# Earlier weights for the first pair, and an earlier eviction of the ninth product, in a one-core hybrid block kernel

## The reference, cut to what matters

```python
h = rmsnorm(x, norm_pre) * (1.0 + scale) + shift
proj = h @ w_in                       # 1024 x 1024 times 1024 x 6144
u_pool, z_pool, u_ssm, z_ssm, g_pool, g_ssm = split(proj)
y_pool = causal_pool_mixer(u_pool, pool_w, pool_scale) * silu(z_pool)
y_ssm = s5_mixer(u_ssm, ...) * silu(z_ssm)   # complex-diagonal state space
merged = sigmoid(g_pool) * (y_pool @ w_branch_pool) + sigmoid(g_ssm) * (y_ssm @ w_branch_ssm)
return x + gate * rmsnorm(merged @ w_out, norm_post)
```

## Time and profile before

| | |
|---|---|
| device time, median of 3 (lowest, highest) | 975.13 us (974.8, 975.58) |
| the profiled execution: its own time | 974.41 us |
| the profiled execution: span from first to last instruction | 972.6 us |
| PE busy | 943.0 us (97%) |
| DVE busy | 653.0 us (67%) |
| ACT busy | 349.7 us (36%) |
| POOL busy | 45.3 us (5%) |
| mean granted clock of TensorE | 0.996 |
| bytes moved | 168.27 MB, mean 173 GB/s |

### The profile page before, as it was taken

How to read it: one execution, slowest core, us unless ns; L and a number is a source line. 1 busy time by engine, 2 the same in 40 slices (tenths; PEclk the granted TensorE clock), 3 DMA queues, 4 the chain that set the end, 5 groups by cost and what they waited for, 6 DMA issues and landing times.

```text
span 972.6 us, 11610 instructions
## 1 busy us (share of the span) xinstructions
PE 943.0 (97%) x4448; PEld 790.7 (81%) x4448; DVE 653.0 (67%) x914; ACT 349.7 (36%) x406; POOL 45.3 (5%) x82
## 2 busy tenths in 40 slices
PE   3999979999999999999999999999999999999997
PEld 3888858888888888888888888888888888787885
DVE  5988977999888868767887667663344444455233
ACT  5741351322443343644554544631122231133111
POOL 0019700000000000000000000000000000000000
PEclk9999989999999999999999999999999999999999
DMA  9753173544445569667567554896543255322222
GB/s 349 287 160 101 73 257 110 190 155 152 152 159 187 185 209 231 213 181 206 174 181 217 152 159 121 277 332 234 174 156 110 103 209 202 129 87 87 87 87 87
DMA packets 95687, 168.27 MB, mean 173 GB/s; under 512 B 37648, under 2 KB 54160, under 8 KB 95632
## 3 DMA queue, kind: packets, MB, share of 16 engines
q1 hardware_dynamic: 86272, 163.07, 50.4%
q10 hardware_dynamic: 9360, 4.46, 2.1%
HBM read 118.21 MB, written 49.28 MB: 172 GB/s over the span
## 4 chain that ended last, share of the span: by engine, by line
PE 87%; POOL 5%; DMA 3%; DVE 2%; ACT 2%; SPq 1%; issue 1%; DVEq 0%; ACTq 0%; POOLq 0%
PE ps L1860 48%; PE ps L1967 17%; PE ps L2068 8%; PE psb L1967 4%; PE ps L2014 2%; PE psb L2003 1%; PE psa L1989 1%; PE psb L2001 1%; DMA raw<-in_wstream 1%; PE psa L1936 1%; DMA coef_d<-coef 1%; POOL coef L482 1%; POOL coef L481 1%; POOL coef L479 1%; DMA pair_raw<-in_wstream 1%
## 5 line engine op out<-in xcount | busy, mean ns | idle before, releaser
L1860 PE MATMUL ps<-bop,w_hi 128*128 128x512 f32 x1312 | 352.5, 391 | 0.7 <-DVE bop L1360 0.7
L1860 PEld LDWEIGHTS ps<-bop,w_hi 128*128 128x128 f32 x1312 | 245.5, 188 | 51.5 <-issue 1.3
L1860 PE MATMUL ps<-bop,w_lo 128*128 128x512 f32 x656 | 202.2, 389 | 0.0
L1860 PEld LDWEIGHTS ps<-bop,w_lo 128*128 128x128 f32 x656 | 123.2, 188 | 25.6
L1312 DVE TENSOR_TENSOR w_lo<-raw,w_hi 128x1024 fp32r<-128x1024 f32 x49 | 60.6, 1236 | 61.0 <-ACT w_hi L979 60.8
L979 ACT ACTIVATE w_hi<-raw 128x1024 fp32r<-128x1024 f32 x49 | 51.7, 1057 | 89.6 <-PE ps L1860 80.4
L1967 PE MATMUL ps<-bop,r_hi 128*128 128x512 f32 x208 | 65.7, 398 | 5.8 <-ACT gt L1047 5.8
L1967 PE MATMUL ps<-t_hi,r_hi 128*128 128x512 f32 x140 | 55.3, 395 | 0.0
L1967 PE MATMUL ps<-t_hi,r_lo 128*128 128x512 f32 x140 | 54.6, 390 | 0.0
L1967 PE MATMUL ps<-t_lo,r_hi 128*128 128x512 f32 x140 | 54.6, 390 | 0.0
L1967 PEld LDWEIGHTS ps<-bop,r_hi 128*128 128x128 f32 x208 | 40.0, 193 | 14.6 <-issue 6.2
(11 more groups left out here) (311 smaller groups left out, 1522.8 us busy)
## 6 DMA issues: line engine op xcount, KB each, us to landing
raw<-in_wstream SPq DMA_DIRECT2D x58, 512.0 KB, 5.4
pair_raw<-in_wstream SPq DMA_DIRECT2D x22, 512.0 KB, 4.6
ada<-in_w_ada SPq DMA_DIRECT2D x16, 512.0 KB, 11.5
x_tok<-in_x SPq DMA_DIRECT2D x8, 512.0 KB, 6.3
gs_d<-gt SPq DMA_DIRECT2D x8, 512.0 KB, 5.0
win_d<-win_new SPq DMA_DIRECT2D x8, 512.0 KB, 3.2
wout_d<-wout_new SPq DMA_DIRECT2D x8, 512.0 KB, 5.6
wout<-wout_d SPq DMA_DIRECT2D x8, 512.0 KB, 3.8
```

The costliest lines, as they stand in the source:

```text
L1860: last = mm(ps[slot(u)][:, f * HALF:f * HALF + HALF], a[:, k, :], b(k, f), start=k == 0 and q == 0, stop=k == KT - 1 and q == 2)
```

## The change

The weights of pair 0 get a place of their own, `pair_first`, over `rt[0]` and `rt[1]`. Those tiles are first written as results of pair 0, when its weights have been read; before, `wx_lo` lies there, which the third product (gs 2) reads last. So `load_pair(0)` now waits for the third product, stands behind the store of gs 4, and the stores of gs 5 and gs 6 stand between it and the store of the coefficients. `load_pair(1)` comes right behind that store, and `load_cf(0)` and `load_cfp(0)` behind a wait for it. `load_pair(2)`, the first into `pair_raw0`, waits for the coefficients' store and no longer for the reads of pair 0. The high and low parts of P1 and P2 still go to the addresses of `coef`, so ACT waits for `coef_stored` there. On ACT they move ahead of `t_high(2)`, and the `evac` of zs 0 moves ahead of the high parts of P6 and P5. On DVE the low parts of P1 and P2 move ahead of `t_low(1)`, the `tabled` wait, `t_sums(3)` and `t_low(2)`; `t_low(3)` moves behind `sum2`.

```diff
+        pair_first = at("pair_first", [P, 2, KT, P], rt_at)
+        def pair_weights(j):
+            return pair_raw[j % 2] if j else pair_first
...
             def load_pair(j):
                 if j == 0:
-                    sp.wait_ge(coef_stored, 16)
+                    sp.wait_ge(mm_done, JOB[USES[2]] + 1)
                 elif j == 1:
                     for s in range(2):
                         sp.wait_ge(raw_free[s], (len(FIRST) + 1 - s) // 2)
+                elif j == 2:
+                    sp.wait_ge(coef_stored, 16)
                 else:
                     pair_read(j - 2)
                 for s in range(2):
-                    sp.dma_start(pair_raw[j % 2][:, s, :, :], ...)
+                    sp.dma_start(pair_weights(j)[:, s, :, :], ...)
...
             load_w(8)
             store_gs(4)
+            load_pair(0)
+            store_gs(5)
+            store_gs(6)
             sp.wait_ge(coef_ready, 2)
             sp.wait_ge(tabled, 1)
             sp.dma_start(coef_d.rearrange("b p f -> p b f"),
...
-            store_gs(5)
-            store_gs(6)
-            load_pair(0)
+            load_pair(1)
+            sp.wait_ge(coef_stored, 16)
             load_cf(0)
             load_cfp(0)
-            load_pair(1)
             store_gs(7)
...
                 if s is None:
                     act.wait_ge(pair_in[j % 2], 32 * (j // 2) + 32)
+                    if j == 0:
+                        act.wait_ge(coef_stored, 16)
...
-            t_high(2)
             pair_high(0, P1)
             pair_high(0, P2)
+            t_high(2)
             t_high(3)
+            act.wait_ge(gs_stored[0], 16 * 4)
+            evac(("zs", 0), gt[0][:, :], ACT.Silu)
             pair_high(0, P6)
             pair_high(0, P5)
-            act.wait_ge(gs_stored[0], 16 * 4)
-            evac(("zs", 0), gt[0][:, :], ACT.Silu)
             pair_high(0, P3)
             pair_high(0, P4)
             pair_high(0, P7)
...
             t_sums(2)
-            t_low(1)
-            dve.wait_ge(tabled, 1)
-            t_sums(3)
-            t_low(2)
...
             pair_low(0, P1)
             pair_low(0, P2)
-            t_low(3)
+            t_low(1)
+            dve.wait_ge(tabled, 1)
+            t_sums(3)
+            t_low(2)
+            dve.wait_ge(coef_stored, 16)
             sum1(0)
             sum2(0)
+            t_low(3)
             sum4(0)
             for i in (P6, P5, P3, P4):
                 pair_low(0, i)
```

More of the change, by code:

```diff
@@ L696, in load_pair @@
                 for s in range(2):
-                    sp.dma_start(pair_raw[j % 2][:, s, :, :], wstream_d[HOST.index((kind, a + s))]).then_inc(pair_in[j % 2], 16)
+                    sp.dma_start(pair_weights(j)[:, s, :, :], wstream_d[HOST.index((kind, a + s))]).then_inc(pair_in[j % 2], 16)
             def store_gs(n):
@@ L1085, in pair_high @@
                     act.wait_ge(mm_done, JOB[FIRST[-1 if o < 6 else -2]] + 1)
-                u = pair_raw[j % 2]
+                u = pair_weights(j)
                 src = {P1: u[:, 0, 0:4, :], P2: u[:, 0, 4:8, :], P4: u[:, 1, 4:8, :]}.get(i)
@@ L1492, in quarter @@
             def quarter(j, s, k):
-                return pair_raw[j % 2][:, s, k:k + 4, :].rearrange("p k m -> p (k m)")
+                return pair_weights(j)[:, s, k:k + 4, :].rearrange("p k m -> p (k m)")
             def pair_slot(j, i):
```

## The result

The changed kernel takes 970.72 us (median of 6 runs, 967.56 to 971.48) against 975.36 us of the kernel before (6 runs): ratio 0.9948, 95% interval 0.9933 to 0.9964. It is faster by 4.6 us, where 7.1 us were forecast. The profiled execution took 970.14 us, its span is 968.4 us, 4.2 us under the 972.6 us of before. The range that was to hold 8 in 10 ended at 970.6 us. The median lies 0.1 us above it as it stands, and inside it, at 970.1 us, if the ratio is applied to the 975.13 us from which the forecast started.

A forecast was written before the change was run, and what follows sets the result against it. TensorE bounds the kernel, stopped before P2 by a late eviction, then slowed by its clock. 5.16 us from P2's earlier start plus 1.93 us from the clock make 7.1 us: 975.13 to 968.0 us, 8-in-10 range 966.8 to 970.6.

The forecast's parts named there:

- What bounds the kernel: Whole kernel: TensorE is nearly always busy, so time won at its stop before P2 arrives in full at the end.
- The sum: Pair 0: P2 starting 5.16 us sooner plus 1.93 us from the clock gives 7.1 us.
- Loads, P1, ScalarE's and VectorE's rows: Ahead of P2: early loads hidden, P1 behind the ninth product, ACT's first high part at 124.34, P2 at 135.5.
- The landing of the coefficients: Coefficients' store before pair 0: issued at 116.2, takes 8.07 us, lands at 124.3; bounds 1 us sooner, 2.6 later.
- case (b): Before P2 and P6: DVE's row longer or coefficients late by 1 to 2.6 us; time 969 to 970.6; chance 0.13.
- The clock: Stop ahead of P2 shrinks to 2.2 us, short enough to keep the clock at 1.00; 1.93 us won.
- Case (a): Stop ahead of P2: clock falls in the shorter stop too; gain 3.7 to 5.4 us, 969.7 to 971.4; chance 0.12.
- P6 and the covers behind it: Pairs 0 and 1: P6 at 138.35 with 0.3 us cover; later covers of 1.3 and 0.8 us hold.
- Case (c): Pairs 0 and 1: DVE becomes the bound, costing at most 4.7 us; time up to 972.7; chance 0.04.
- (d): Coefficients' store: landing slips by more than 7.1 us and the kernel gets slower, 977.1 at 9.1 us; chance 0.02.
- (e): Ninth product's eviction: something else holds it, so the change does nothing; time 975; chance 0.01.

The follow-up runs named there:

- e4: Changed kernel with the ScalarE and VectorE orders of before, except the ninth product's eviction stays ahead of P6 and P5: 964.93 us, ratio 0.9897.
- e7: Changed kernel with a one-column Silu behind t_high(2), so the table loads where ScalarE idles: 968.29 us, ratio 0.9927.
- e5: Changed kernel with load_pair(1) moved behind the wait for the coefficients' store, so nothing is queued behind that store: 968.91 us, ratio 0.993.
- e2: Kernel before with one edit, the ninth product's eviction ahead of the high parts of P6 and P5 on ScalarE: 967.59 us, ratio 0.9925.
- e9: Kernel before with the changed orders of ScalarE and VectorE, loads and stores untouched: 975.74 us, ratio 1.0004.
- e6: Changed kernel with 12 more matmuls between P1 and P2 of pair 0, into a bank nobody reads: 969.03 us, ratio 0.9934.
- e10: Changed kernel with VectorE's order alone put back to that of before: 966.05 us, ratio 0.9904.
- e1: Changed kernel run again without edit, as yardstick, against the kernel before: 969.74 us, ratio 0.994.
- e8: Changed kernel with the ninth product's eviction moved ahead of t_high(3) too: 969.89 us, ratio 0.9941.

## Why the prediction was right in direction and too large in size

*What bounds the kernel* and that the gain arrives at the end: right, except that the slice with the dip is the sixth and not the seventh, on which nothing rests. The changed kernel's P6 starts 4.1 us sooner, the span is 4.2 us shorter. In e4 P6 starts 9.3 us sooner, and the span is 9.5 us shorter.

*The sum.* Forecast: P2 starts 5.16 us sooner and runs 1.93 us faster, 7.1 us together. The changed kernel's profile: P2 starts 140.67 - 136.93 = 3.74 us sooner and runs 4.78 - 4.41 = 0.37 us faster, 4.1 us together. So 1.4 us are missing in the first term and 1.56 us in the second.

*Loads, P1, ScalarE's and VectorE's rows*: the durations held. From the first high part to P2 were forecast 11.2 us (124.34 to 135.5) and passed 11.2 us (125.75 to 136.93). P1 started right behind the ninth product. The table switch cost 1.28 us and no drain, in the changed kernel and in e7; the Trainium skill's 2.66 us (ScalarE: Activation LUTs, section What ACT_TABLE_LOAD costs) would have put P2 1.4 us later, and the measurement decides.

*The landing of the coefficients* was mis-sized. Term: 8.07 us from 116.2. Measured: 8.91 us from 116.75. Of the 1.4 us, 0.5 is the later issue, which differs from one profile to the next: 116.0 to 117.0 us in the ten with the changed loads, 116.2 to 116.3 us in the three others. Whether the change has a small part in it is open. The other 0.84 us is the megabyte of weights behind the store: the nine profiles that have it there read 8.9 us, e5 takes it away and reads 8.07; in the order of SP of before, with a megabyte of gate stores behind, e2 and e9 read 8.09 and 8.08. The bounds held it, the value taken did not. The range's case (b) had 0.13 of the chance.

*The clock* was the step that failed. The prediction put the new stop at 2.2 us and took it as short enough, 1.93 us won. The stop was 3.44 us, and the clock fell. But e5 shows that 2.29 us was not safe either: the two rows on which the step rested, a stop of 1.26 us that cost nothing and a clock that fell 3.3 us into a stop, do not say what happens once TensorE has resumed. In the changed kernel 2 of 11 runs (967.56, 967.42) look untouched, 9 do not. From the profile, 1.56 us of P2's 4.41 us are the clock's (2.85 us was P1's pace); the filler of e6, which kept the clock up, gives 1.60 us. The single runs at 971.3 to 971.5 fit a clock that stayed down longer, as before the change; their mean granted clock was 0.994 to 0.996, that of the run at 967.56 was 0.999. But the run at 969.54 shows 0.996 too, and no profile of such a run was taken, so that is argued and not shown. Case (a) had priced this at 969.7 to 971.4 us and given it 0.12; in most runs the clock fell as it says, in the profile for half of the 6.8 us, which is the milder end of (a). That the median lies inside the bounds of (a) owes something to the late coefficients, which (a) did not include.

The prediction cited the Trainium skill here (TensorE: Matmul & The Clock Gate, section A second HAM failure mode: psum-queue depth-cycling). That section tells of small idles that recur between groups of matmuls and make the clock swing. This case has single stops, so its traces bear on it only in part: single stops of 2.29, 2.87, 3.17 us lost the clock, a stop of 1.66 us did not.

*P6 and the covers behind it*: right. P6's low part was ready in time, no bank wait shows in pairs 0 and 1, VectorE's two waits shrank from 4.45 us to the 1.62 us at 159. `c11` ended at 149.10, with P3 starting at 152.25. Case (c) did not come up, nor (d), nor (e).

*What the prediction did not say*: that the change holds edits of opposite worth. The eviction alone is worth 7.5 us (e2), VectorE's new order costs 3.7 us (e10), and with that order and late weights the whole gain of the eviction is gone (e9). The rows to see it were before it. VectorE used its wait for the weights for `t_low(1)`, `t_sums(3)` and `t_low(2)` in the kernel before; the change keeps that wait and moves the work behind it, onto the path to the eviction. The prediction laid out the new row on VectorE with the right durations, and never asked what the change would do without it.

## What to carry to other kernels

Work that stands ahead of a wait in a hand-written order is free as long as the wait is there; moved behind the wait, it is on the path. Before moving operands earlier, look which single instruction releases the stalled engine and what stands ahead of it in its queue for other reasons: here one eviction moved past two copies gave 7.5 us, more than the whole rearrangement. In these profiles every stop of TensorE of 2.29 us or more was followed by a stretch at half clock, so such a stop cost more than its length, by 1.3 to 1.9 us where P2 stood behind it.

## What the runs showed of the hardware

- The clock can fall after TensorE has resumed (changed kernel: P2 from 136.93, clock down near 137.6; e5: P2 from 136.36, down near 137.1). In e1 and e8 it fell inside the stop (near 136.2 and 138.4). The profiles with one stop of 2.29 to 3.46 us were at 0.50 for 3.4 us, the two with a stop of 5.85 and 6.75 us (before and e9) for 6.8 us. What it cost depended on how much of this fell on work. Of the thirteen profiles the clock fell in each whose longest stop here was 2.29 us or more, and in none whose longest was 1.66 us or less. A profile is one execution: single runs of the same kernels, as 967.14 and 967.15 in e5, look as if the clock had held.
- What is queued behind a large store matters by kind: 2.6 MB took 8.07 to 8.09 us with nothing (e5) or with 1 MB of stores from on-chip memory behind it (before, e2, e9), and 8.9 us in the nine profiles with 1 MB of loads behind it (8.91 us in the changed kernel's, 8.94 us in e8's). The mechanism was not looked into.
- The table load took 1.28 us, and the next instruction of ScalarE started 0.01 us behind it (changed kernel, e7).
